# State-space groups: the clipped distances of eight heads on ScalarE, and two heads to an operation in exponential and masked product

## Reference

```python
scores = jnp.einsum('bclgn,bcsgn->bgcls', cc, bc)
mmat = scores[:, :, None] * segsum_decay(a_cs)     # exp(a_cs[l] - a_cs[s]) where s <= l, else 0
y_diag = jnp.einsum('bghcls,bcsghp->bclghp', mmat, x)
...
y = y + d_skip.astype(jnp.float32)[:, None] * x32
y = y.reshape(b, seq, D_INNER).astype(h.dtype) * jax.nn.silu(z)
y = rmsnorm(y.reshape(b, seq, SSD_GROUPS, D_INNER // SSD_GROUPS), ...)
```

## Time and profile before

| | |
|---|---|
| median of 3 runs | 1154.95 us (1153.59 to 1155.33) |
| the profiled execution | 1155.13 us, span 1153.3 us |
| TensorE busy | 1122.8 us (97%) |
| weight loads (PEld) busy | 1082.8 us (94%) |
| VectorE busy | 978.2 us (85%) |
| ScalarE busy | 710.8 us (62%) |
| GpSimd busy | 34.7 us (3%) |

### The profile page before, as it was taken

How to read it: one execution, slowest core, us unless ns; L and a number is a source line. 1 busy time by engine, 2 the same in 40 slices (tenths; PEclk the granted TensorE clock), 3 DMA queues, 4 the chain that set the end, 5 groups by cost and what they waited for, 6 DMA issues and landing times.

```text
span 1153.3 us, 25636 instructions
## 1 busy us (share of the span) xinstructions
PE 1122.8 (97%) x9126; PEld 1082.8 (94%) x9126; DVE 978.2 (85%) x1785; ACT 710.8 (62%) x1109; POOL 34.7 (3%) x64
## 2 busy tenths in 40 slices
PE   8989999999999999999999999999999999999997
PEld 7989999999899999999999989999899999999997
DVE  7877999998998998989999799999996777766667
ACT  6556656666556456656566577888866556554454
POOL 0000000000000110000000000000000000000000
PEclk9989999999999999999999999999999999999999
DMA  7534677675666867866766537457546566656551
GB/s 280 184 113 155 210 239 237 220 257 184 207 242 258 296 247 245 293 196 231 239 217 210 166 115 252 148 187 195 172 145 232 170 213 210 211 186 195 193 190 37
DMA packets 73041, 235.73 MB, mean 204 GB/s; under 512 B 7424, under 2 KB 16640, under 8 KB 72848
## 3 DMA queue, kind: packets, MB, share of 16 engines
q1 hardware_dynamic: 64304, 203.86, 53.2%
q0 software_dynamic: 8528, 30.98, 7.9%
q10 hardware_dynamic: 144, 0.02, 0.0%
HBM read 233.73 MB, written 1.09 MB: 204 GB/s over the span
## 4 chain that ended last, share of the span: by engine, by line
PE 70%; DVE 19%; issue 5%; ACT 4%; DMA 1%; DVEq 1%; SPq 0%; ACTq 0%
PE ps L242 21%; PE ps L243 20%; PE ps L244 20%; DVE w_lo L234 5%; PE ps L274 3%; DVE arena L2004 2%; PE ps L276 2%; DVE arena L496 1%; ACT w_hi L229 1%; DVE arena L933 1%; DMA w_raw<-stream 1%; DVE arena L1992 0%; PE ps L1668 0%; DVE arena L1404 0%; DVE arena L968 0%
## 5 line engine op out<-in xcount | busy, mean ns | idle before, releaser
L234 DVE TENSOR_TENSOR w_lo<-w_raw,w_hi 128x1024 fp32r<-128x1024 f32 x381 | 461.1, 1218 | 11.7 <-ACT w_hi L229 5.8
L242 PE MATMUL ps<-a_hi,w_hi 128*128 128x256 f32 x1656 | 463.2, 280 | 5.0 <-DVE w_lo L234 3.6
L243 PE MATMUL ps<-a_lo,w_hi 128*128 128x256 f32 x1656 | 455.4, 275 | 0.0
L244 PE MATMUL ps<-a_hi,w_lo 128*128 128x256 f32 x1656 | 455.4, 275 | 0.0
L229 ACT ACTIVATE w_hi<-w_raw 128x1024 fp32r<-128x1024 f32 x381 | 390.6, 1048 | 20.0 <-PE ps L244 12.2
L242 PEld LDWEIGHTS ps<-a_hi,w_hi 128*128 128x128 f32 x1656 | 317.6, 192 | 12.3 <-issue 5.7
L243 PEld LDWEIGHTS ps<-a_lo,w_hi 128*128 128x128 f32 x1656 | 317.8, 192 | 0.6 <-issue 0.2
L244 PEld LDWEIGHTS ps<-a_hi,w_lo 128*128 128x128 f32 x1656 | 318.0, 192 | 0.0
L242 PE MATMUL ps<-b_both,w_hi 128*128 128x256 f32 x560 | 156.5, 279 | 2.0 <-DVE b_both L993 1.0
L243 PE MATMUL ps<-b_both,w_hi 128*128 128x256 f32 x560 | 154.2, 275 | 0.0
L244 PE MATMUL ps<-b_both,w_lo 128*128 128x256 f32 x560 | 154.1, 275 | 0.0
(11 more groups left out here) (315 smaller groups left out, 1682.3 us busy)
## 6 DMA issues: line engine op xcount, KB each, us to landing
w_raw<-stream SPq DMA_DIRECT2D x381, 512.0 KB, 4.1
arena<-ada POOLq DMA_DIRECT2D x48, 512.0 KB, 5.6
c_both<-cum_rows POOLq DMA_DIRECT2D x4, 1024.0 KB, 7.3
arena<-x SPq DMA_DIRECT2D x2, 512.0 KB, 4.6
con<-consts SPq DMA_DIRECT2D x1, 1024.0 KB, 5.7
arena<-row_cols POOLq DMA_DIRECT2D x2, 512.0 KB, 5.4
arena<-c_rows POOLq DMA_DIRECT2D x1, 512.0 KB, 4.4
out<-arena SPq DMA_DIRECT2D x2, 256.0 KB, 2.2
```

Source lines behind the costliest of these rows:

```text
L234: dve.tensor_tensor(w_lo[:, s % RING], w_raw[:, s % RING], w_hi[:, s % RING].bitcast(F32), ALU.subtract).then_inc(w_lo_ready, 1)
L242: pe.matmul(o, wh, xh, start=start, stop=False, skip_group_check=shared)
L243: pe.matmul(o, wh, xl, start=False, stop=False, skip_group_check=shared)
L244: return pe.matmul(o, wl, xh, start=False, stop=stop, skip_group_check=shared)
```

## The change

All heads' distances are now made by ScalarE as ReLUs, each pair right ahead of its exponential. The pair's exponential is one operation of 768 columns over two neighbouring places of `seen`, and so is the masked product on VectorE, which reads the scores twice by a broadcast. VectorE's `gaps` is gone, with the semaphore `gap_ready`; its waits (`rows_landed`, `yssd_ready`, `y_done`) move to ScalarE, ahead of the ReLUs of steps 8, 9 and 10. `first_gaps` now counts 16 per group, `exp_done` and `seen_ready` one per pair, and the load of the next group's rows waits for `first_gaps` alone.

```diff
--- before.py
+++ after.py
@@ -1526,6 +1526,8 @@
         y_seen = area(4 * SEQ + 2 * SEEN)
         y_f = y_seen[:, 0:4 * SEQ].rearrange("p (a t) -> p a t", a=4)
         seen = [y_seen[:, c:c + SEEN] for c in (4 * SEQ, 4 * SEQ + SEEN, 0, SEEN)]
+        seen_pair = [y_seen[:, c:c + 2 * SEEN] for c in (4 * SEQ, 0)]
+        PAIRS = GROUP_HEADS // 2
         cum_rows = nc.dram_tensor("cum_rows", (GROUPS, GROUP_HEADS * SEQ), F32, kind="Internal").ap()
         cum_all = c_hi.bitcast(F32)
         cb = area(SEEN)
@@ -1549,8 +1551,8 @@
         tap_done, conv_done, act_done, z_done, u_done = (sem(n) for n in ("tap_done", "conv_done", "act_done", "z_done", "u_done"))
         cb_ready, cb_masked, own_ready, own_copied = sem("cb_ready"), sem("cb_masked"), sem("own_ready"), sem("own_copied")
         x_turned, x_tok_ready = sem("x_turned"), sem("x_tok_ready")
-        rows_stored, rows_landed, first_gaps, gap_ready, exp_done, seen_ready, y_done = (
-            sem(n) for n in ("rows_stored", "rows_landed", "first_gaps", "gap_ready", "exp_done", "seen_ready", "y_done"))
+        rows_stored, rows_landed, first_gaps, exp_done, seen_ready, y_done = (
+            sem(n) for n in ("rows_stored", "rows_landed", "first_gaps", "exp_done", "seen_ready", "y_done"))
         yz_ready, ysq_ready, ysum_ready, inv_s_ready = (sem(n) for n in ("yz_ready", "ysq_ready", "ysum_ready", "inv_s_ready"))
         z_silu, yn_ready, yhi_ready, yssd_ready = sem("z_silu"), sem("yn_ready"), sem("yhi_ready"), sem("yssd_ready")
         gate_ready, pooled_ready, pooled_hi, pooled_operand = (sem(n) for n in ("gate_ready", "pooled_ready", "pooled_hi", "pooled_operand"))
@@ -1657,7 +1659,7 @@
                         pe.transpose(ps[:, 5 + b, 3 * P:4 * P], cv[:, 5, b * P:(b + 1) * P], ident).then_inc(x_turned, 1)
 
                 def head_pair(q):
-                    pe.wait_ge(seen_ready, in_group(2 * q + 2, 8, g, it))
+                    pe.wait_ge(seen_ready, in_group(q + 1, PAIRS, g, it))
                     if q == 0:
                         pe.wait_ge(x_tok_ready, in_group(2, 2, g, it))
                     if q == 2:
@@ -1789,15 +1791,12 @@
                         c = slice(0, SEQ) if b == 0 else slice(SEQ, SEEN)
                         h = GROUP_HEADS * g + k
                         h = slice(h, h + 1) if it is None else bass.ds(it * GROUP_HEADS + h, 1)
-                        row = cum_all[:, k, b * P:SEQ] if g else ps[:, 7, k * SEQ + b * P:(k + 1) * SEQ]
+                        row = cum_all[:, k, b * P:SEQ] if g or k > 1 else ps[:, 7, k * SEQ + b * P:(k + 1) * SEQ]
                         act.activation(seen[k % 4][:, c], row, ACT.Relu, bias=cum_tok[:, b, h], scale=-1.0).then_inc(first_gaps, 1)
 
-                def exps(k):
-                    if k < 2:
-                        act.wait_ge(first_gaps, in_group(2 * k + 2, 4, g, it))
-                    else:
-                        act.wait_ge(gap_ready, in_group(2 * k - 2, 12, g, it))
-                    act.activation(seen[k % 4], seen[k % 4], ACT.Exp, scale=-1.0 if k < 2 else 1.0).then_inc(exp_done, 1)
+                def decays(p):
+                    act.wait_ge(first_gaps, in_group(4 * p + 4, 4 * PAIRS, g, it))
+                    act.activation(seen_pair[p % 2], seen_pair[p % 2], ACT.Exp, scale=-1.0).then_inc(exp_done, 1)
 
                 def first_distances():
                     if g:
@@ -1807,9 +1806,15 @@
                     gaps(0)
                     gaps(1)
 
-                def decays(k):
-                    exps(k)
-                    exps(k + 1)
+                def later_distances(p):
+                    if p == 1:
+                        act.wait_ge(rows_landed, in_group(16, 16, g, it))
+                        if g:
+                            act.wait_ge(yssd_ready, in_group(1, 1, g - 1, it))
+                    else:
+                        act.wait_ge(y_done, in_group(2 * p - 2, GROUP_HEADS, g, it))
+                    for k in (2 * p, 2 * p + 1):
+                        gaps(k)
 
                 def gate_silu():
                     act.wait_ge(z_done, in_group(4, 4, g, it))
@@ -1827,7 +1832,8 @@
                         if g:
                             tail(j, g - 1, it)
                     if 8 <= j < 11:
-                        decays(2 * (j - 7))
+                        later_distances(j - 7)
+                        decays(j - 7)
                     if j == 10:
                         gate_silu()
                     used(j)
@@ -1974,22 +1980,10 @@
                 def heads_of(c, n=1):
                     return slice(c, c + n) if it is None else bass.ds(it * GROUP_HEADS + GROUP_HEADS * g + c, n)
 
-                def gaps(k):
-                    if k == 2:
-                        dve.wait_ge(rows_landed, in_group(16, 16, g, it))
-                    if k == 2 and g:
-                        dve.wait_ge(yssd_ready, in_group(1, 1, g - 1, it))
-                    if k >= 4:
-                        dve.wait_ge(y_done, in_group(k - 3, 8, g, it))
-                    for b in range(NB):
-                        c = slice(0, SEQ) if b == 0 else slice(SEQ, SEEN)
-                        dve.tensor_scalar(seen[k % 4][:, c], cum_all[:, k, b * P:SEQ], cum_tok[:, b, heads_of(k)], 0.0,
-                                          ALU.subtract, ALU.min).then_inc(gap_ready, 1)
-
-                def weighted(k0):
-                    for k in (k0, k0 + 1):
-                        dve.wait_ge(exp_done, in_group(k + 1, 8, g, it))
-                        dve.tensor_tensor(seen[k % 4], seen[k % 4], cb, ALU.mult).then_inc(seen_ready, 1)
+                def weighted(p):
+                    dve.wait_ge(exp_done, in_group(p + 1, PAIRS, g, it))
+                    both = seen_pair[p % 2].rearrange("p (i t) -> p i t", i=2)
+                    dve.tensor_tensor(both, both, cb.unsqueeze(1).broadcast_to((P, 2, SEEN)), ALU.mult).then_inc(seen_ready, 1)
 
                 for j in range(GRP):
                     if g and j != 7:
@@ -2027,15 +2021,9 @@
                     if g and j == 7:
                         tail(j, g - 1, it)
                     if j > 8:
-                        weighted(2 * (j - 8))
-                    if j in (9, 10):
-                        gaps(2 * (j - 7))
-                        gaps(2 * (j - 7) + 1)
+                        weighted(j - 8)
                     if j >= 7:
                         split_lo(dve, S_GRP + GRP * g + j + 3, it, GRP)
-                    if j == 7:
-                        gaps(2)
-                        gaps(3)
                     if j == 11:
                         skip(0, g, it)
                         skip(1, g, it)
@@ -2498,8 +2486,7 @@
             pool.wait_ge(rows_stored, 16)
             for g in range(GROUPS):
                 if g:
-                    pool.wait_ge(first_gaps, 4 * g)
-                    pool.wait_ge(gap_ready, 12 * g)
+                    pool.wait_ge(first_gaps, 16 * g)
                 pool.dma_start(cum_all, cum_rows[g:g + 1].rearrange("a (h t) -> a h t", t=SEQ).broadcast_to((P, GROUP_HEADS, SEQ))).then_inc(rows_landed, 16)
             pool.wait_ge(mod_ready, 1)
             pool.dma_start(row_cols[0].rearrange("(m p) -> p m", p=P), mod[:, 5 * NT:6 * NT], allow_slow_non_contiguous=True).then_inc(rows_stored, 16)
```

## The result

The changed kernel takes 1160.51 us (median of 5 runs, 1160.11 to 1160.97), the kernel before, run beside it, 1154.41 (1153.37 to 1155.33): a ratio of 1.0056, 95% interval 1.0043 to 1.0069. It is slower by 6.1 us, where 1160.6 was forecast. Its profiled execution took 1160.51 us, with a span of 1158.7.

A forecast was written before the change was run, and what follows sets the result against it. The order of work around a ScalarE-VectorE ring was taken to bound the kernel, no engine having much to give. 1.9 for group 0 plus 3 x 1.2 gave +5.5 us on 1155.13, so 1160.6, range 1154 to 1163.

The forecast's parts named there:

- The ring: Loop through ScalarE's gaps(0), decay stages, last product, VectorE's queue from `skip(2)` to tile 5's taps, `silu(5)`; period 40.42 us.
- waits at `silu(5)`: TensorE's loader stops at L1657 before `turn`'s last two transposes: 5.3 us in four waits; TensorE's waits were to grow.
- VectorE's relief: Twelve subtractions fewer and merged products free VectorE of 3.0 us per group, which becomes idle time before the exponentials.
- t0 to `skip(2)`: From gaps(0)'s start on ScalarE to VectorE's `skip(2)` in a loop group: 20.92 us instead of 19.73, +1.19.
- a stage: ScalarE's steps 8 to 10: four ReLUs, exponential, eviction and split take 3.45 us, where stages came every 3.0.
- Group 0: First group, outside the loop: `skip(2)` 19.81 us after gaps(0) starts instead of 17.67, +2.14, or +1.9 after absorption.
- the stretch `skip(2)` to t0: From `skip(2)` to the next group's gaps(0): 20.69 us in the loop, holding nothing of the change.
- The absorption of 0.2 behind group 0: The stretch after the first group's `skip(2)` takes 20.91 against 20.69 us, so its +2.14 becomes +1.9.
- Rival B: Evens out: stages about 3.05 us, by four ReLUs at 1.1 or a much cheaper exponential; 1155 us, chance 0.10.
- Rival A: VectorE's freed time counts if four ReLUs take 1.03 us or less: about -8, 1147 us; chance 0.10.
- Rival C: ReLU needs another table than Exp, so later stages reload tables: 31 us more, 1191 us; chance 0.02.
- The stop before `head_pair(1)`: TensorE's loader waits at L1668 for masked products of heads 2 and 3: keeps 0.9 of its 0.95 us.

The follow-up runs named there:

- relu_half: The change with the ReLUs of heads 2 to 7 over half of their columns, the rest left out: 1156.94 us, ratio 1.0034.
- relu_eighth: The change with the ReLUs of heads 2 to 7 over an eighth of their columns, the rest left out: 1153.63 us, ratio 0.9998.
- relu_only: The change with exponentials and masked products left one per head (384 columns), all ReLUs on ScalarE: 1159.01 us, ratio to before 1.0048.
- product_apart: The change with the masked product as two operations of 384 columns, the exponential still merged: 1159.88 us, ratio 1.0046.
- shared kernels: Kernel before, ScalarE making later pairs' even-head distances, VectorE odd, product merged: 1152.01 us; also with step 11's split ahead of z's Silu: 1150.32 us.
- the change again: The changed kernel measured and profiled once more with no edit: 1161.35 us, ratio 1.0059.
- merge_only: Kernel before with each pair's exponential and masked product merged to 768 columns, VectorE keeping its subtractions: 1154.21 us against 1153.57, ratio 1.0001.
- split_first: The change with ScalarE's split for step 11 made ahead of the Silu of z instead of behind it: 1158.76 us, ratio 1.0041.

## Why the prediction was right

- *The ring and its place*: shown. The waits at `silu(5)` grew, all of VectorE's relief turned into waits for ScalarE, and the length of the ReLUs alone moves the total (relu_half, relu_eighth).
- *t0 to `skip(2)`*: 20.92 was worked out, 21.00 measured; periods in the loop 41.79 against 41.6. Four ReLUs took 1.48, a stage 3.47 against 3.45. *Group 0*: 19.81 worked out, 19.97 measured.
- *Terms that were off*: the stretch `skip(2)` to t0 took 21.04 behind group 0, where 20.69 had been taken, and 20.79 in the loop, where it was to stay as it was. The absorption of 0.2 behind group 0 was right (20.67 in relu_only, 20.68 in product_apart); on top of it come the widened gaps between taps, 0.57 us in all, for which the sum had nothing. Together with the small misses (0.16 in group 0, 0.06 in each of the others) this makes 6.4 instead of 5.5.
- *Rival B's threshold*: four ReLUs at 1.1 us were to be even. Half the columns, 1.17 us, is still 3.4 us slower, and an eighth, 0.92 us, is even (1153.63 against 1153.99). Between their middle columns of 142.10 and 139.22 the 139.57 of before lies at 0.95 us. So B's 1.1 was too high. A's 1.03 fits a turn of the loop: between 40.83 us with half the columns and 40.10 with an eighth the 40.42 of before lies at 1.03 us. Group 0 is 0.6 us longer even with an eighth, which draws the whole down to 0.95.
- *Rival A* failed as said: VectorE's 3 us were worth nothing while ScalarE could not keep pace. Its mechanism is real, though, as the shared kernels show.
- *Rival C* is out: 4 table loads for Exp in the groups of the changed kernel as in the one before, though 48 of its 64 ReLUs come behind an exponential. The Trainium skill (ScalarE: Activation LUTs, Table sets: the hidden batching unit) says of ReLU that every set has it; for Exp's set this trace agrees.
- *The stop before `head_pair(1)`*: 0.9 us as said, in two groups of the first profile and in three of the second.
- *What the sum hid*: it was made on one profiled execution, and 1160.6 fell on the median partly by luck. That execution of before had 2.3 us in the attention part that the first profile of the change had not (half-clock there), and the change has 1.1 to 1.3 us behind the groups that were not in the sum. In this pair of profiles 5.5 + 0.9 + 1.3 - 2.3 = 5.4 us, the difference of the spans. Over the runs the medians are 6.1 apart, and 6.9 for the change again. Seen so, the base that I took, 1155.13, was 0.7 above the median of before beside the change, and the 5.5 added to it 0.6 too small; the two nearly cancel. What the clock does varies from run to run: the change has the attention part's stretch in its second profile and not in its first, and the runs of before at a mean clock of 0.998 took 1152.6 to 1153.7 us, those at 0.995 or 0.996 took 1153.6 to 1155.3 (22 runs of the kernel before, taken beside merge_only).

## To carry to other kernels

When two engines are both nearly full and hand work to each other in a fixed order, look at the stage, not at the sums: moving 3 us to the engine with 20% idle time cost 6 us, because its idle time stood right where the moved work's inputs came from. Compare both engines' work per stage before and after, as the larger sets the pace: ScalarE and VectorE had 2.2 and 3.0 us before, 3.5 and 2.1 after the change, and 2.8 and 2.5 with the heads shared. Moving all cost 6 us, and moving half, with the product merged, won 2. Merging two operations behind a producer on the same engine saved 0.07 us here and cost 0.12, as the merged one waits until the last input has been written.

## What the hardware showed beyond that

TensorE's granted clock drops to half (1.2 GHz) in a few stretches, at different places in different executions. Leaving out the one at the very end, where TensorE has no work left, these are the three of the first profile of the change, with busy time and clock (the column before the DMA share is the clock):

```profile
685.70:689.10 3.40, 3.40 (x19) 3.40 (x18) 3.26 (x8) 1.36 (x2) 0.95 (x1) 0.50 0.62 180
733.50:736.90 3.40, 3.40 (x16) 3.40 (x17) 3.40 (x7) 3.37 (x7) 0.00 (x0) 0.50 0.10 41
866.60:870.00 3.40, 3.40 (x18) 3.40 (x18) 3.37 (x6) 0.56 (x2) 0.00 (x0) 0.50 0.79 261
```

The kernel before has one such stretch of 6.8 us in the attention part:

```profile
65.90:72.70 6.80, 6.79 (x28) 6.44 (x29) 4.84 (x16) 3.59 (x12) 1.36 (x1) 0.50 0.26 77
```

The last of the three begins 1.4 us after TensorE stood still for 2.86 us at the eleventh gate slab, and the second profile of the change has its like at 867.4, behind 2.87 us. But product_apart stood still for 2.86 us at the same slab and relu_only for 2.91, and neither has such a stretch there:

```profile
864.80:868.20 3.40, 3.40 (x31) 3.40 (x32) 3.37 (x5) 1.91 (x4) 0.00 (x0) 1.00 0.62 180
```

So in two profiles a long stop goes before the drop, and in two others the same stop brings none. Inside the groups a stretch at half clock costs little or nothing, as the ring and not TensorE sets the time there (145.97 with one such stretch inside, 145.96 without). Behind the groups it goes with about 0.6 us: the rest is 320.4 and 320.3 with it, 319.7 in relu_half, relu_eighth and split_first, which have no such stretch there. The 0.6 from there to the 319.1 of before are the longer row of the last output transfers (see product_apart). What decides whether a half-clock stretch comes was not tried.
